# Attention batches taken two by two in a hybrid decoder: scores of both, transposes apart, values of both

## The reference

```python
q = (x @ w_q + b_q).reshape(Bsz, nb, BLK, KVH_B, GRP_B, DH_B)
s = jnp.einsum('bnqkgd,bnpkd->bnkgqp', q, k2).astype(jnp.float32) * (DH_B ** -0.5)
s = jnp.where(valid[None, :, None, None], s, -jnp.inf)
sk = sinks.astype(jnp.float32).reshape(KVH_B, GRP_B)[None, None, :, :, None, None]
mx = jnp.maximum(jnp.max(s, axis=-1, keepdims=True), sk)
p = jnp.exp(s - mx)
p = p / (jnp.sum(p, axis=-1, keepdims=True) + jnp.exp(sk - mx))
o = jnp.einsum('bnkgqp,bnpkd->bnqkgd', p.astype(v2.dtype), v2)
return o.reshape(Bsz, S, NH_B * DH_B) @ w_out + b_out
```

## Time and profile before

| what | us |
|---|---|
| median of 3 runs (lowest, highest) | 2009.98 (2009.53, 2010.36) |
| profiled execution, its own time | 2009.53 |
| span of that execution | 2007.9 |
| PE busy | 1983.1 (99%) |
| DVE busy | 1322.9 (66%) |
| ACT busy | 920.6 (46%) |
| POOL busy | 1203.7 (60%) |
| from 1118 to 1285: PE, DVE, ACT busy | 166.2, 122.4, 97.2 of 167.0 |

### The profile page before, as it was taken

One profiled execution on the slowest core, in us unless ns is written; L12 is line 12 of the kernel. 1 busy time (PEld: TensorE's weight loads), 2 busy tenths in 40 slices (PEclk: granted clock), 3 DMA queues, 4 the chain that ended last, 5 costly groups with the idle time before them and its releaser, 6 DMA issues.

```text
span 2007.9 us, 28849 instructions
## 1 busy us (share of the span) xinstructions
PE 1983.1 (99%) x10000; PEld 1655.8 (82%) x10000; DVE 1322.9 (66%) x1745; ACT 920.6 (46%) x1928; POOL 1203.7 (60%) x1055
## 2 busy tenths in 40 slices
PE   9999999999999999999999999999999999999998
PEld 8898988888888888878888777788888888888886
DVE  7764552688777777454666676779666666645567
ACT  6434333365545545432245455456445454432233
POOL 5443322656888987656674211363978888746566
PEclk9999999999999999999999999999999999999999
DMA  7574435835877778695853122563677667597673
GB/s 209 163 261 168 167 146 205 311 123 168 260 243 246 245 243 252 237 383 182 276 180 73 44 85 74 187 198 97 219 254 234 227 231 239 193 352 278 216 263 135
DMA packets 293652, 415.01 MB, mean 207 GB/s; under 512 B 39160, under 2 KB 216328, under 8 KB 293520
## 3 DMA queue, kind: packets, MB, share of 16 engines
q1 hardware_dynamic: 256752, 307.58, 46.9%
q10 hardware_dynamic: 35344, 100.98, 13.9%
q0 software_dynamic: 1424, 4.77, 0.8%
HBM read 259.09 MB, written 154.17 MB: 206 GB/s over the span
## 4 chain that ended last, share of the span: by engine, by line
PE 90%; DVE 5%; issue 2%; ACT 2%; DMA 1%; POOL 0%; SPq 0%; ACTq 0%; POOLq 0%; DVEq 0%
PE ps L2425 22%; PE ps L2427 22%; PE ps L2426 22%; PE ps L2336 8%; PE ps L2338 4%; PE ps L2776 2%; PE ps L2610 1%; PE ps L2611 1%; PE ps L2607 1%; PE ps L2737 1%; PE ps L2480 1%; DMA scratch_forms<-prep_forms 1%; DVE forms L1905 1%; PE ps L2796 1%; DVE mats L1806 1%
## 5 line engine op out<-in xcount | busy, mean ns | idle before, releaser
L2425 PE MATMUL ps<-forms,mats 128*128 128x512 f32 x2016 | 788.4, 391 | 7.2 <-ACT part L1389 2.3
L2427 PE MATMUL ps<-forms,mats 128*128 128x512 f32 x2016 | 785.0, 389 | 0.0
L2426 PE MATMUL ps<-forms,mats 128*128 128x512 f32 x2016 | 784.6, 389 | 0.0
L1071 POOL TENSOR_TENSOR mats<-sum_a,mats 128x256 fp32r<-128x256 f32 (+2 forms) x384 | 404.8, 1058 | 363.5 <-ACT mats L1310 362.3
L2425 PEld LDWEIGHTS ps<-forms,mats 128*128 128x128 f32 x2016 | 378.5, 188 | 92.8 <-issue 14.6
L2427 PEld LDWEIGHTS ps<-forms,mats 128*128 128x128 f32 x2016 | 378.5, 188 | 79.6
L2426 PEld LDWEIGHTS ps<-forms,mats 128*128 128x128 f32 x2016 | 378.6, 188 | 76.8
L1829 DVE TENSOR_TENSOR X<-ps,X 128x512 f32<-128x512 f32 x390 | 268.2, 690 | 192.3 <-PE ps L2427 190.2
L1310 ACT ACTIVATE mats<-sum_a 128x256 fp32r<-128x256 f32 (+2 forms) x392 | 201.6, 516 | 312.2 <-PE ps L2427 295.1
L1806 DVE TENSOR_TENSOR mats<-stream_raw,mats 128x256 fp32r<-128x256 f32 (+2 forms) x302 | 280.3, 930 | 20.1 <-ACT mats L1310 19.3
L1310 ACT ACTIVATE mats<-stream_raw 128x256 fp32r<-128x256 f32 (+2 forms) x302 | 156.6, 519 | 243.6 <-PE ps L2427 241.5
(11 more groups left out here) (257 smaller groups left out, 2644.1 us busy)
## 6 DMA issues: line engine op xcount, KB each, us to landing
forms<-scratch_forms ACTq DMA_DIRECT2D x182, 512.0 KB, 5.4
scratch_forms<-prep_forms SPq DMA_DIRECT2D x161, 512.0 KB, 3.4
stream_raw<-in_w_gate_up_dram SPq DMA_DIRECT2D x88, 512.0 KB, 5.4
scratch_forms<-head_forms SPq DMA_DIRECT2D x49, 512.0 KB, 3.0
scratch_hidden<-hidden SPq DMA_DIRECT2D x84, 256.0 KB, 5.5
prep_raw<-in_w_down_dram SPq DMA_DIRECT2D x38, 512.0 KB, 5.6
stream_raw<-scratch_hidden SPq DMA_DIRECT2D x32, 512.0 KB, 4.6
forms<-scratch_forms SPq DMA_DIRECT2D x28, 512.0 KB, 5.4
```

What stands on the lines that cost most here:

```text
L1071: pool.tensor_tensor(blocks(m[:, q, 1, :], it.width), stream_source(it, q), blocks(m[:, q, 0, :].bitcast(F32), it.width), ALU.subtract).th ...
L2425: mm(dst, ah, bh, start=OPENS[q] and k == 0, stop=False, skip_group_check=True)
L2426: mm(dst, ah, bl, start=False, stop=False, skip_group_check=True)
L2427: m = mm(dst, al, bh, start=False, stop=k == w - 1, skip_group_check=True)
```

## The change

A duo is two batches, 2d and 2d+1. PE's order for duo d becomes: scores of 2d and 2d+1, transposes of 2d-2, the first part of the duo's query steps, transposes of 2d-1, the last two query steps, values of 2d-2 and of 2d-1. The first part has 5 steps in duos 1, 3, 5, 7, 9, 10 and 12, 6 steps in 2, 4, 6, 8, 11 and 13, 4 in duo 14 (which has no second part) and none in duo 15, where products 1 and 2 stand in its place. The values of the two batches go to the two halves of bank 7, which ACT copies in one go (512 columns), and only the even batch's values wait for that copy. Products 3, 4 and 5 stand before the last values, product 0 behind the transposes of duo 14. On DVE and ACT the steps follow in the order of the loops below.

In the first head, the load of the head row is issued earlier on SyncE's queue, its first two sums stand before the seventh tile's norm on GpSimd, the high and low halves 1 and 2 stand ahead of the gates, high half 5 ahead of the queries' copy, and the gate rows' transposes one column step (three matmuls) later.

```diff
-        FIRST_LO_AT = {BATCHES - 7: 0, BATCHES - 4: 3, BATCHES - 1: 6}
-        FIRST_ADD_AT = {BATCHES - 2: (0,), BATCHES - 1: (1,), BATCHES: (3, 4), BATCHES + 1: (5,)}
+        DUOS = BATCHES // 2
+
+        def duo_steps(duo):
+
+            both = query_steps(2 * duo) + query_steps(2 * duo + 1)
+            at = len(both) - min(2, len(query_steps(2 * duo + 1)))
+            return both[:at], both[at:]
+
+        FIRST_HI_AT = {DUOS - 4: (0, 1), DUOS - 3: (2, 3), DUOS - 2: (4, 5), DUOS - 1: (6,)}
+        FIRST_LO_AT = {DUOS - 3: 0, DUOS - 2: 3, DUOS - 1: 6}
...
+            sp.wait_ge(lo_ready, len(VK))
+            load_head_row(0)
...
-            store_head_forms(0, (0, 1))
+            store_head_forms(0, (0, 1, 2))
             load_unit(1, 2)
-            store_head_forms(0, (2, 3, 4, 5, 6))
+            store_head_forms(0, (3, 4, 5, 6))
...
-            rstd_of_tiles(0, range(7))
+            rstd_of_tiles(0, range(6))
+            head_sums(0, (1, 2))
+            rstd_of_tiles(0, (6,))
             gain(Unit(3))
             rstd_of_tiles(0, (7,))
             for j in (4, 5):
                 gain(Unit(j))
-
-            head_sums(0, (1, 2, 3, 4))
+            head_sums(0, (3,))
...
+            head_sums(0, (4,))
...
-                    head_row_hi(0, 0)
+                    for q in (0, 1):
+                        head_row_hi(0, q)
+                if t == TT - 1:
+                    head_row_hi(0, 2)
             write_hi(Unit(5))
             v_out(TT - 2)
-            for q in (1, 2):
-                head_row_hi(0, q)
...
-            for q in (3, 4):
+            for q in (3, 4, 5):
...
+            for duo in range(DUOS + 2):
+                r = 2 * duo
+                if duo < DUOS:
+                    scores_in(r)
+                    queries_out(duo_steps(duo - 1)[1] if duo else ())
+                e = r - 4
+                if e >= 0:
+                    act.wait_ge(oT_ready, e + 2)
...
+                    act.activation(yT[:, ue, 2 * me * P:(2 * me + 4) * P], ps[:, 7, :], ACT.Copy).then_inc(oT_copied, 2)
+                if duo < DUOS:
+                    exponentials(r)
+                    queries_out(duo_steps(duo)[0])
+                    scores_in(r + 1)
+                    exponentials(r + 1)
+                for q in FIRST_HI_AT.get(duo, ()):
+                    stream_hi(first_out, q)
...
-            head_row_lo(0, 0)
+            for q in (0, 1):
+                head_row_lo(0, q)
             write_lo(Unit(4))
             write_lo(Unit(5))
+            head_row_lo(0, 2)
...
+            for duo in range(DUOS):
+                r = 2 * duo
+                if duo == DUOS - 1:
+                    add_product(first_out, 0)
+                if duo:
+                    mask_probs(r - 2)
+                merge_scores(r)
+                if duo:
+                    scale_probs(r - 1)
+                    mask_probs(r - 1)
+                scale_probs(r)
+                merge_scores(r + 1)
+                if duo in FIRST_LO_AT:
+                    stream_lo(first_out, FIRST_LO_AT[duo])
+            for q in (1, 2):
+                add_product(first_out, q)
+            mask_probs(BATCHES - 2)
+            scale_probs(BATCHES - 1)
+            add_product(first_out, 3)
+            mask_probs(BATCHES - 1)
+            for q in (4, 5):
...
-                        if half == 0 and k == 4:
+                        if half == 0 and k == 5:
...
-                    c = slice(i * P, (i + 1) * P)
+                    c = slice((2 * (e % 2) + i) * P, (2 * (e % 2) + i + 1) * P)
...
-                if e:
+                if e and e % 2 == 0:
...
+            def probs_transposes(e):
+
+                pe.wait_ge(probs_scaled, e + 1)
+                if e:
+                    pe.wait_ge(pt_ready, 2 * e)
+                for j in range(4):
+                    p = nc.tensor.transpose(ps[:, 6, j * P:(j + 1) * P], Sm[:, e % 2, j, 0:P], ident[:])
+                p.then_inc(probsT_ready, 1)
+
+            query_columns(query_steps(-1))
+            for half in range(2):
+                pe.wait_ge(bank_free[6 + half], uses.before[6 + half])
+            for duo in range(DUOS):
+                r = 2 * duo
+                scores_of(r)
+                scores_of(r + 1)
+                if duo:
+                    probs_transposes(r - 2)
+                query_columns(duo_steps(duo)[0])
+                if duo == DUOS - 1:
+                    pe.wait_ge(bank_free[1], uses.before[1])
+                    product(first_out, 1)
+                    product(first_out, 2)
+                if duo:
+                    probs_transposes(r - 1)
+                query_columns(duo_steps(duo)[1])
+                if duo == DUOS - 2:
                     pe.wait_ge(bank_free[0], uses.before[0])
                     product(first_out, 0)
+                if duo == DUOS - 1:
                     pe.wait_ge(merged, BATCHES - 1)
                     product(first_out, 3)
+                if duo:
                     values_of(r - 2)
+                    values_of(r - 1)
+            probs_transposes(BATCHES - 2)
+            product(first_out, 4)
+            probs_transposes(BATCHES - 1)
+            product(first_out, 5)
+            values_of(BATCHES - 2)
+            values_of(BATCHES - 1)
```

More of the change, by code:

```diff
@@ L700, in load_gains, with load_head_row @@
                              ).then_inc(gains_loaded, 16)
+            def load_head_row(r):
+                w = (w_out[0], wdn[0])[r % 2]
+                for f in range(2):
+                    sp.dma_start(head_raw[f][:], w[(r // 2) * (2 * P) + f * P:(r // 2) * (2 * P) + (f + 1) * P, :]
+                                 ).then_inc(head_loaded, 16)
             for t in range(2):
@@ new lines, in scores_in @@
+                if r >= 2:
+                    act.wait_ge(probsT_ready, r - 1)
+                act.activation(Sm[:, r % 2, :, P].rearrange("p (a i) -> p a i", a=2),
+                               sink[:, u::PAIRS].unsqueeze(2).to_broadcast([P, 2, 2]), ACT.Copy).then_inc(sink_set, 1)
+                act.wait_ge(scores_ready, r + 1)
+                s0 = 2 + 2 * (r % 2)
+                first = int(m == 0)
+                act.activation(Sm[:, r % 2, first::1 + first, 0:P],
+                               ps[:, s0:s0 + 2, :].rearrange("p a (i c) -> p (a i) c", i=2)[:, first::1 + first, 0:P],
+                               ACT.Copy).then_inc(prev_copied, 1)
@@ new lines, in scores_in, with exponentials, queries_out @@
+                if m == 0 and 0 < u < PAIRS - LEAD:
+                    write_hi(Unit(U_Q + u) + LEAD)
+            def exponentials(r):
+                act.wait_ge(negmax_ready, r + 1)
+                for j in range(4):
+                    act_j = act.activation(Sm[:, r % 2, j], Sm[:, r % 2, j], ACT.Exp, bias=st[:, r % 4, 0, j:j + 1],
+                                           accum_out=st[:, r % 4, 1, j:j + 1])
+                act_j.then_inc(probs_ready, 1)
+            def queries_out(steps):
+                for v, half, k in steps:
+                    if k == KT - 1:
+                        query_half(v, half, half, Kq[half] + v)
@@ L2050, in _ @@
             dve.tensor_tensor(windows[:, 1], gc[:], gl[:], ALU.subtract).then_inc(gate_dve, 1)
-            for q in (1, 2):
-                head_row_lo(0, q)
             for _ in range(2):
@@ L2742, in out_values, with query_columns @@
                 p.then_inc(oT_ready, 1)
-            def query_columns(r):
-                for v, half, k in query_steps(r):
+            def query_columns(steps):
+                for v, half, k in steps:
                     un = Unit(U_Q + v)
```

170 lines of the change are left out of this document (49 added, 121 removed).

## The result

| what, in us | before | after |
|---|---|---|
| median of 6 runs each (lowest, highest) | 2009.76 (2008.87, 2011.94) | 2017.4 (2016.5, 2018.07) |
| profiled execution: span | 2007.9 | 2015.6 |
| first scores | 1118.28 | 1117.15 |
| first scores to the first scores of duo 15 | 151.86 | 150.96 |
| first scores to the last product | 881.71 | 890.55 |

The changed kernel is slower, by a ratio of 1.0036 (95% interval 1.0026 to 1.0047). Three stretches add up to it. The first scores come 1.1 us earlier (third row), and from there to duo 15 fifteen duos take 0.9 us less (fourth row). The loss lies behind that: the time to the last product (fifth row) is 8.8 us longer, so from duo 15 on 9.7 us are lost.

The account below looks back on a forecast made before the run. PE's own instruction stream was taken to set the time. Terms -8.6 + 9.1 + 6.7 - 0.5 = +6.7 on the profiled 2009.53 gave 2016.2, as a median 2016.6 us, range 2013 to 2020.

Parts of the forecast that it names:

- Part 1: Loop of the attention stage: fewer changes of shape on PE save 0.57 us per duo, 8.6 over duos 0 to 14.
- Part 2: Loop: PE's second transposes of a duo wait for DVE's late scaling, 9.1 us in all (7.5 to 10.5).
- Part 3: End of the attention stage: PE's waits for DVE and a load cost 6.7 us net (bounds 3.5 and 8.5).
- Part 4: First head: shorter waits for gate rows and keys against more waiting at the gates, -0.5 us (-1.5 to +2).
- rival (d): First head: head-row sums on GpSimd wait for a late load, delaying transposes 2 to 4 us; 2019 us, chance 0.08.
- (a): Loop: DVE's chain is not late for the transposes, but the end still costs; 2007.6 us, chance 0.10.
- (c): Loop and end: DVE's work fits under the columns, only the saved shape changes count; 2001 us, chance 0.07.
- (b): End of the stage: the loop's waits come, but the end costs only about 2 us; 2012 us, chance 0.13.
- (e): Loop: scores to transposes costs as much as scores to columns, handovers a little later; 2019 us, chance 0.07.

Follow-up runs that it names:

- The repaired kernel: The changed kernel with scaling between masks and merging, weight split and both halves of form 6 moved, values of batch 30 behind product 4: 2001.99 us, ratio 0.9965.

## Why the prediction was right

It was right in mechanism and total, +7.7 against +6.7 by the spans, but the sizes were off in opposite directions: the loop by -1.4, the head by -0.6, the end by +3.0. That the total came so close is in part luck. By the steps:

- **Part 1, changes of shape.** The loop without waits (the kernel with the scaling between masks and merging) shows the saving: duos 1 to 14 take 8.4 us less than the same pairs of batches before, 0.60 each, against 0.57. The change that no trace had shown, scores to transposes, was taken at 0.05 and came out at 0.06, in the first transpose's own gap (0.165 instead of 0.109). From the last score to the transposes pass 0.31 us, as from scores to columns before. That is 0.09 more than between scores, but the prediction's 0.18 inside the scores held it already: its 1.06 us run up to the first column. The Trainium skill (TensorEngine Tiling (Array Packing), Key Properties) states that a change of tiling mode drains TensorE. The trace agrees in so far as the 0.31 is the same in front of transposes and of columns; the slow start behind it is not, 0.06 against 0.10, so the saving lies above the 0.51 for each duo that I had drawn from that rule. Duo 0 is shorter by 0.86, but about 0.4 of this is not saved: the transposes of batch 0 now stand behind the scores of duo 1, and so everything is one set of transposes later up to the end of the stage.
- **Part 2, the waits for the scaling.** Gaps from the last column to the transposes, less the usual 0.23: 0.30 in duos 1, 3, 5, 7, 9 (predicted 0.35), 1.15 in 2, 4, 6 (1.57), 0.70 in 10 and 12 (0.66), 1.38 in 14 (1.35), none in 8, 11, 13. Sum 7.7 against 9.1, plus 0.6 for slower first transposes behind 11 waits. Nearly the whole error is the weight split, 0.4 in each of three duos, which take 11.35 and not about 11.8: I took 1.6 from the earlier trace rows, and it takes 1.22 in all three. The row of batch 4 was stretched, see the last section. The exponentials end 2.2 us into duo 6 (at 1178.20) and not when it starts, but that is still ahead of the scaling, so it cost nothing here. The waits vanish when only the scaling is moved: shown.
- **Part 3, the end.** Waits: 1.34 for 1.05 predicted, 3.66 for 3.9, 3.0 for 2.6, and none for the 0.55 of transposes 31. Their sum is 8.0 for 8.1. In the 1.34, the scaling in front of the transposes took 1.22 us beside GpSimd instead of 0.69 (last section), which the sum did not have. Transposes 31 start at 1284.86, behind the end of the scaling at 1284.62, only because product 4 ran at the slow clock; at full speed PE would have been there at an estimated 1284.2 and waited about 0.4. The chain named for product 4 (exponentials, high half, low half, sums) and that for product 6 (the load behind the values of batch 30) were both shown by undoing them. What the part left out is the price of idling itself: 3.1 us of slower matmuls at 1.2 GHz. The end cost 9.7, not 6.7: 8.0 of waits, 3.1 of slow matmuls and the 0.4 of transposes that moved there, less 1.1 of waits of before (0.48, 0.4, 0.2) and 0.7 that is left for changes of shape (0.5 predicted).
- **Part 4, the head.** The waits for kT (1.0) and the gate rows (0.8) went, the windows' shrank by 0.3 where I had put 0.4 more, and two waits for the normed tiles came, 1.1 us. This is rival (d), at about half of the least it was given, but not by the late landing that it names. The head row landed 2.9 us after GpSimd got there, and that alone cost nothing: GpSimd began the sums at 27.32, and the seventh tile's norm had its own input only at 27.38. What held the norm up are the two sums themselves, 2.6 us; it ran at 29.93 instead of 27.43. With 0.3 for one more new wait these make -0.7; the first scores come 1.1 earlier in this pair of profiles, against -0.5 predicted, and single profiles differ by more than that.

In one line: loop -0.9 (predicted +0.5), end +9.7 (+6.7), head -1.1 (-0.5). Rivals (a) and (c) fell with the waits seen; (b) fell at product 4; (e) wanted 0.11 for scores to transposes and later handovers, and neither came. The repaired kernel, at 2001.99, is what (c) described at 2001.

What stays open: what decides whether the clock falls behind an idle near 3 us, and the head's gain to better than 1 us.

## What to carry to other kernels

Grouping work of one shape on TensorE pays what the count of shape changes says (0.60 us for each pair of batches here), but it moves the moments at which the other engines' results are wanted, and their queues have to be put in order again for that: here one scaling, moved ahead of a copy and a maximum on DVE, was worth 8.4 us in the loop. A queue can be wrong on either side: behind work that is not urgent the scaling was late, and ahead of work whose input was there it blocked. And at a seam between stages, ask for each sum and load what stands ahead of it on its engine without being needed first.

## What the runs showed of the hardware

**Idles cost twice.** Behind idles of PE of 3.66 and 3.0 us the granted clock fell to 1.2 GHz for about 3.4 us, with products at 0.42 us instead of 0.23; 3.1 us of slower matmuls by the estimate above. Over all profiles of the end of this stage, it fell behind every idle from 3.66 to 4.46 us (seven profiles); between 2.98 and 3.30 us it fell five times, and twice (3.19 and 3.25) it did not. The length of the idle alone does not decide it.

**A DVE operation with both inputs in SBUF is held up by GpSimd's.** The scaling took 0.69 us alone. In the kernel with the scaling at the head it took 1.63 beside GpSimd's addition (1175.19 to 1177.59) and ended 0.55 after the addition's end; in the kernel with the scaling between masks and merging it took 1.02 and ended again 0.55 after it:

```profile
1175.61 1.02 DVE L2336 TENSOR_TENSOR S_merged<-S_merged,softmax_cols 128x512 f32<-128x512 f32 x1
```

```profile
1173.67 2.41 POOL L1253 TENSOR_TENSOR X<-X,b_out_row 128x1024 f32<-128x1024 f32 x1 [7.74 <-PE ps L2818]
```

The masks, which have one input in PSUM, kept their 0.69 beside that second addition, and so did the maximum of the earlier trace rows, which has a single input in SBUF. The Trainium skill (SBUF — State Buffer, SBUF: two separate sides) calls the pair of ports that the two engines share an exclusive lock and not a split of bandwidth; by that an operation is held until the other's end, and the rows agree. Such an addition also stood beside the weight split of the earlier trace rows in the kernel before, from which the prediction took a price 0.4 too high. The next split of the same kernel, with nothing of GpSimd beside it, took 1.22:

```profile
1136.92 2.45 POOL L1242 TENSOR_TENSOR X<-X,b_out_row 128x1024 f32<-128x1024 f32 x1 [10.85 <-PE ps L2776]
1159.91 1.22 DVE L1759 TENSOR_TENSOR w_split<-raw,w_split 128x1024 fp32r<-128x1024 f32 x1
```

In the changed kernel the same happened in front of the transposes of batch 29. Again the scaling ended 0.55 us after GpSimd's operation:

```profile
1273.52 1.22 DVE L2336 TENSOR_TENSOR S_merged<-S_merged,softmax_cols 128x512 f32<-128x512 f32 x1
```

```profile
1273.47 0.72 POOL L1070 TENSOR_TENSOR sum_a<-sum_a,stream_raw 128x256 f32<-128x256 f32 x1
```
